# Identity products on TensorE between the last output product and the first expert rows

## What is computed

```python
g_idx = jnp.argmax(softmax(ht @ w_group + b_group), axis=-1)        # 1 of 4 groups
e_sel = (ht @ w_expert + b_expert).reshape(T, 4, 8)[tok, g_idx]
top_v, top_i = lax.top_k(e_sel, 2)                                  # 2 of its 8 experts
top_w = softmax(top_v) * g_p[:, None]
...
yr = (jax.nn.silu(xb @ w_gate[e]) * (xb @ w_up[e])) @ w_down[e]     # blocks of 128 rows of one expert
y  = zeros.at[row_tok].add(yr * row_w[:, None])
```

## Time and profile before

| | |
|---|---|
| time, median of 3 runs | 2466.1 us (2462.89 to 2468.29) |
| the profiled execution's own time | 2466.4 us |
| its span from first to last instruction | 2464.8 us |
| mean granted TensorE clock over the span | 0.964 |
| busy share of PE, DVE, ACT, POOL | 92%, 57%, 49%, 31% |

### The profile page before, as it was taken

One profiled execution on the slowest core, in us unless ns is written; L12 is line 12 of the kernel. 1 busy time (PEld: TensorE's weight loads), 2 busy tenths in 40 slices (PEclk: granted clock), 3 DMA queues, 4 the chain that ended last, 5 costly groups with the idle time before them and its releaser, 6 DMA issues. The chain is left out here.

```text
span 2464.8 us, 36702 instructions
## 1 busy us (share of the span) xinstructions
PE 2273.8 (92%) x11342; PEld 1827.2 (74%) x11342; DVE 1392.7 (57%) x3012; ACT 1220.0 (49%) x1644; POOL 758.1 (31%) x685
## 2 busy tenths in 40 slices
PE   7799999997999999999979995799999999999980
PEld 6688889996777777777658884677888888788760
DVE  4353431105777677667346676576655566666663
ACT  4211111114777777777634443565645555656553
POOL 0000000004887787877501112222222222222220
PEclk9999999998999999999989996899999999999995
DMA  8653334225543454434046444699887888988957
GB/s 272 172 205 111 111 136 117 64 65 133 137 113 86 96 135 109 100 87 120 18 162 197 125 129 155 210 356 356 270 273 247 265 259 266 326 290 270 330 147 289
DMA packets 211558, 450.48 MB, mean 183 GB/s; under 512 B 21633, under 2 KB 56577, under 8 KB 207874
## 3 DMA queue, kind: packets, MB, share of 16 engines
q1 hardware_dynamic: 191410, 378.91, 47.0%
q0 software_dynamic: 17744, 61.96, 10.0%
q10 hardware_dynamic: 2304, 8.39, 1.5%
HBM read 347.44 MB, written 101.76 MB: 182 GB/s over the span
## 5 line engine op out<-in xcount | busy, mean ns | idle before, releaser
L1532 DVE TENSOR_TENSOR gu_lo<-gu_raw,gu_hi 128x2048 fp32r<-128x2048 f32 x128 | 293.8, 2295 | 117.7 <-issue 80.7
L719 DVE TENSOR_SCALAR_CACHE_REDUCE p_ring<-ps_s 128x512 f32<-128x512 f32 (+6 forms) x352 | 277.6, 793 | 117.7 <-PE ps_s L790 104.0
L659 POOL TENSOR_TENSOR p_ring<-p_ring 128x512 f32<-128x512 f32 (+2 forms) x192 | 334.5, 1742 | 16.0
L684 ACT ACTIVATE p_ring<-p_ring,shift 128x1152 f32<-128x1152 f32 (+15 forms) x256 | 305.7, 1196 | 17.5 <-DVE shift L735 17.5
L827 PE MATMUL ps_o<-aT,v_st 128*128 128x512 f32 (+3 forms) x640 | 285.5, 530 | 0.0
L673 ACT ACTIVATE aT<-ps_t 128x512 f32<-128x512 f32 (+1 forms) x320 | 169.1, 530 | 164.2 <-PE ps_t L812 163.0
L1609 PE MATMUL ps_g<-gu_hi,xT_lo 128*128 128x512 f32 x720 | 236.0, 409 | 7.5 <-DVE xT_lo L1547 7.5
L1472 ACT ACTIVATE gu_hi<-gu_raw 128x2048 fp32r (+1 forms) x128 | 238.0, 1915 | 9.9 <-PE ps_g L1609 5.1
L1609 PE MATMUL ps_g<-gu_lo,xT_hi 128*128 128x512 f32 x720 | 228.1, 398 | 0.0
L1609 PE MATMUL ps_g<-gu_hi,xT_hi 128*128 128x512 f32 x720 | 227.9, 398 | 0.0
L656 POOL TENSOR_SCALAR p_ring<-p_ring,coef 128x512 f32<-128x512 f32 (+2 forms) x192 | 168.0, 875 | 122.3 <-DVE coef L748 121.9
(11 more groups left out here) (206 smaller groups left out, 4243.1 us busy)
## 6 DMA issues: line engine op xcount, KB each, us to landing
gu_raw<-in_moe_w_gate SPq DMA_DIRECT2D x128, 512.0 KB
gu_raw<-in_moe_w_up SPq DMA_DIRECT2D x128, 512.0 KB
d_raw<-in_moe_w_down SPq DMA_DIRECT2D x64, 1024.0 KB
qk<-stage SPq DMA_DIRECT2D x64, 512.0 KB, 2.8
q_first<-qk SPq DMA_DIRECT2D x64, 256.0 KB, 5.1
q_second<-qk SPq DMA_DIRECT2D x64, 256.0 KB, 5.1
w_raw<-in_w_in_blocks POOLq DMA_DIRECT2D x11, 1024.0 KB, 6.4
k<-qk SPq DMA_DIRECT2D x8, 1024.0 KB, 12.2
```

What stands on the lines that cost most here:

```text
L659: pool.tensor_tensor(p0(r, c0, c1), p0(r, c0, c1), p1(r, c0, c1), ALU.add).then_inc(mixed, 1)
L684: nc.scalar.activation(p, p, ACT.Exp, bias=shift[:, r % 8, m:m + 1], accum_out=sums[:, r % 8, m:m + 1]).then_inc(raised, 1)
L719: ins = nc.vector.tensor_scalar(p(r, k0, k0 + far), ps_s[:, c % 2, 0:far], SCALE, None, ALU.mult, ALU.max, accum_out=top[:, r % 4, m, col: ...
L1532: nc.vector.tensor_tensor(gu_lo[:, j * GC:(j + 1) * GC], raw(half, j), gu_hi[:, j * GC:(j + 1) * GC].bitcast(F32), ALU.subtract).then_inc( ...
```

## The change

TensorE multiplies the 128 x 128 identity, which lies in SBUF for the transposes, by itself, in fp32 and with 128 columns, into the first columns of `ps_a`. Nobody reads the result. `ps_a` is free there: the added wait is for the last reader of the output stage's transposes. The numbers of products are 16 in step 17, 12 in step 18, 24 in step 19, and 56 after the last count. Nothing else is edited.

```diff
+            def fill(count):
+
+                for _ in range(count):
+                    pe.matmul(ps_a[:, 0:P], ident[:, :], ident[:, :], start=True, stop=True)
+
+            FILLS = {TILES + 1: 16, TILES + 2: 12, TILES + 3: 24}
+
             def step(n, par, at):
...
                 else:
+                    if at == TILES + 1:
+                        pe.wait_ge(oT_lo_set, TILES + OT_LO0)
+                    if at in FILLS:
+                        fill(FILLS[at])
                     route(n, at)
                     turn_h2(n, par, at)
 
             steps(pe, step)
             pe.wait_ge(slot_set, TILES + SLOT0)
             pe.matmul(ps_e[:, 0:EXPERTS], ones[:, :], before[:, :], start=True, stop=True).then_inc(counted, 1)
+            fill(56)
```

## The result

| | before | after |
|---|---|---|
| median of 17 runs each | 2465.45 us (2461.07 to 2468.35) | 2471.68 us (2465.68 to 2474.49) |
| ratio of the times | | 1.0023, 95% interval 1.0016 to 1.0031 |
| span of the profiled execution | 2464.8 us | 2470.3 us |
| mean granted TensorE clock | 0.964 | 0.967 |

A forecast was written before the change was run, and what follows sets the result against it. The pipeline's drain was taken as a chain through VectorE, PE and GpSimd. From 2466.4 us, -1.0 + 0.2 - 0.9 - 0.3 = -2.0 gave 2464.4, and a median 0.3 lower 2464.1 us; range 2460.5 to 2468.5.

The forecast's parts named there:

- 56 fills ... I put +0.2: Behind the last count: fills last 13.8 of 14.0 us with 3.6 us at half clock first; +0.2 us put down.
- Do the fills fit?: TensorE's idle times after each count: at full clock all four groups fit, with 3.3, 1.0, 1.9 and 2.0 us to spare.
- -0.9 for turn_x at full clock: Block 0: eight transposes take 0.91 us instead of some 1.8 at half clock; -0.9 us, bounds 0 and -0.9.
- What one fill costs: Each 128-column fp32 identity product on TensorE: 0.215 us at full clock, 0.43 at half.
- The clock falls again in step 17, and comes back in the 12 fills: TensorE: half clock near 1505 in the first route, full again in step 18's fills after 3.6 us of dense work.
- Counts at full clock, -1.0: Tiles 14 and 15: count start to VectorE's place takes 0.75 us, not 1.27; -1.0 us for both.
- The rows of block 1 bound gate_up's gain: Block 0's gate_up 1.7 us faster, but block 1's rows are late; -0.3 us, PE then idle 1 to 2 us.
- The rival "slower": All groups: identity products do not lift the clock, each fill takes 0.43 us; +14.5 us, median 2480.6, chance 0.05.
- The rival "the clock holds all the way": Drain through the first block: full clock throughout; -4.9 us, median 2461.2, chance 0.17.

The follow-up runs named there:

- e6: Kernel before, no fills, but TensorE waits for three split weight slots of expert 0 ahead of its first x_turned increment; 2468.64 us, ratio 1.0025.
- e1: Changed kernel with all 108 products, but TensorE's first x_turned increment moved ahead of the 56 fills; 2462.46 us, ratio 0.9996.
- e5: e1 with 28, 12, 8 plus 30, and 10 products in steps 17 to 20, and 54 behind the last count; 2457.33 us, ratio 0.9983.
- e10: e1 with 28 products in step 17 in place of 16; 2464.43 us beside 2468.5 for the kernel before, ratio 0.9984.
- e2: Changed kernel without the 56 fills, keeping the groups of 16, 12 and 24; 2463.77 us, ratio 0.9999 to the kernel before.
- e4: Changed kernel with 20 products in place of 56 in the last group, x_turned increment still behind it; 2459.47 us, ratio 0.9984.
- e8: e4 with the x_turned increment moved ahead of the last group of 20; 2459.59 us, ratio 0.9987 to the kernel before.
- e7: Changed kernel with only the last group of 56, x_turned increment ahead of it, no fills in steps 17 to 20; 2462.73 us, ratio 1.0001.
- e9: e5 with 20 products in place of 54 behind the last count; 2464.76 us beside 2468.5 for the kernel before, ratio 0.9982.

## Why the prediction was wrong, step by step

- **The step that failed** is the term "56 fills ... I put +0.2", and with it the question "Do the fills fit?". I measured the gap up to TensorE's own next wait, turn_x at 1544.78, and asked only whether the fills end before it. I did not ask which increments stand behind the fills on the queue. There the limit is GpSimd's list load, for which the credit must be given some 5.4 us after the last count (1535.51 - 1530.13) and not 14.0. It came 8.7 us late; with 0.8 gained by the counts and 1.8 by the shorter issue of the gather, 6.4 arrived at turn_x. e6 shows the loss without fills, e1 its absence with them. Even with the credit early the +0.2 was too small: in e1 the 56 fills take 15.16 us, not 13.8, since the clock stayed at half for 5.1 us of them and not 3.6, and turn_x comes 0.8 us later after the last count than before.
- **A knock-on:** my -0.9 for turn_x at full clock fell with it, since the engine idled again, for 5.85 us. In e1, with turn_x in 1.04 us, a part of it is there: turn_x of block 0 starts no earlier than before, yet that of block 1 comes 66.56 us after the route of tile 13, before 67.12.
- **What one fill costs.** 0.215 us predicted. In e5 54 fills last 12.30 us and 12 last 2.92, so one more fill is 0.223. Right within 4%.
- **The clock falls again in step 17, and comes back in the 12 fills.** Right: half from 1503.1, full from 1510.0. The reason was half right. I blamed thin work as much as idleness; in e1 the clock was down 0.7 us before the thin route began, and in e10, with the gap cut to 0.36 us, the same route ran at full clock. The Trainium skill (TensorE: Matmul & The Clock Gate, Why this matters for your kernels) ties the loss to idle gaps between bursts. Step 17 of e1 and of e10 agree with that; the fall of e10 at 1514.9, after a thin route between 0.17 us and 0.7 us of idleness, does not follow from it.
- **Counts at full clock, -1.0:** -0.8 in the profiled execution. e1, e2, e4 and e8 have the same three groups and gave -0.8, +0.4, +0.5 and -0.6: in e2 and e4 the 24 fills began at half clock and lasted 8.3 us, not 7.0, so the count of tile 15 came behind them.
- **The rows of block 1 bound gate_up's gain:** in e1, with gate_up mostly at full clock, PE waited 0.35 us for them. The place was right, the wait smaller than the 1 to 2 us that I named.
- **The rival "slower"** had the right sign and the wrong place. Products of the identity do lift the clock (e7, at 1532.2), so its mechanism is out. Its own threshold was also miscounted: by 0.43 and 0.215 a fill, 56 fills fill 14.0 us once 3.9 us of them run at half clock, not 9; and the first group, 6.9 us at half clock, does not fit its 6.7. The late increment was not among the rivals.
- **The rival "the clock holds all the way"**, -4.9 us, is what e5 does once the gaps are full: 4.2 by the ratio (0.0017 x 2463.3), 5.9 by the medians.

**Left open in part:** why e4 and e8 are 3 to 4 us faster by their medians than e2 and e1. Counted from the route of tile 13, turn_x of block 2 comes 3.2 us earlier than before in e8 and 1.8 in e4, but only 0.7 in e1 and 0.0 in e2. Most of it arises between the blocks: in e4 and e8 turn_x of block 2 came 12.2 and 12.8 us after that of block 1, before 15.6. In e8 the list landed 0.7 us sooner, and the issue of the gather took 0.99 us, before 2.65. GpSimd's rows and VectorE's, first of e8 and then of the kernel before:

```profile
1561.65 0.58 POOL L1437 DMA_DIRECT2D lists<-slots  x1 [8.54 <-PE ps_x L1608]
1566.32 0.99 POOL L1439 DMA_INDIRECT xg<-h_rows,lists  x1 [4.09 <-DMA lists<-slots]
1563.93 2.29 DVE L1545 TENSOR_TENSOR gu_lo<-gu_raw,gu_hi 128x2048 fp32r<-128x2048 f32 x1 [0.70 <-ACT gu_hi L1485]
1566.55 2.29 DVE L1545 TENSOR_TENSOR gu_lo<-gu_raw,gu_hi 128x2048 fp32r<-128x2048 f32 x1 [0.32 <-DVE gu_lo L1545]
```
```profile
1563.87 0.58 POOL L1424 DMA_DIRECT2D lists<-slots  x1 [8.30 <-PE ps_x L1596]
1569.27 2.65 POOL L1426 DMA_INDIRECT xg<-h_rows,lists  x1 [4.82 <-DMA lists<-slots]
1568.76 2.29 DVE L1532 TENSOR_TENSOR gu_lo<-gu_raw,gu_hi 128x2048 fp32r<-128x2048 f32 x1 [0.33 <-DVE gu_lo L1532]
```

The rows show what goes with a long issue: VectorE's splitting of a weight slot (`gu_lo` or `d_lo`, some 2.3 us each). Before, the gather starts inside such a split (1568.76 to 1571.05) and its issue ends at 1571.92, 0.87 us behind it; in e8 it starts in the gap between two. So it is for block 0: before, the gather at 1538.42 starts inside the split of 1538.03 to 1540.32 and ends 0.89 behind it; in the changed kernel it starts at 1545.02, when no split runs, and takes 1.02. The 12 traces have 552 of these gathers. The 345 that start outside a split take 0.99 to 1.02 us, and so do seven that start at its very edge (in its last 0.13 us, and one 0.03 us after it began); the issue of each of the other 200 ends 0.86 to 0.89 us behind the split. No run moved a split on purpose, so that the one waits for the other is read from these rows and not tested. Why the list lands sooner in e8 is open, and e9 does not have this gain: its gather of block 2 starts 0.16 us into a split and takes 2.99.

## What to carry to other kernels

Work that fills an idle engine's gap delays everything behind it on that engine's queue, and semaphore increments that cost nothing are the easiest to miss: list each increment behind the new work, find who waits for it, and take the earliest of these as the end of the gap. Give one-time credits before any such filler. And in step 17 filler meant to hold the clock paid only when it covered the gap nearly whole: 16 products in a gap of 6.7 us gave nothing in that step, 28 gave 2.3 us.

## What the runs showed of the hardware

Products of the identity by itself bring TensorE's clock back: in e7 it had been at half for 29.6 us when the fills began, behind 2.69 us of idleness and one small product, and it rose 4.6 us into them. The issue of one gather of 128 rows on GpSimd took 0.99 to 1.02 us when no weight split ran on VectorE, and otherwise ended about 0.9 us behind the split that ran when it started, so that it took up to 3.1 us. The late gather of block 0 met no split, and was 1.8 us cheaper than the punctual one, which did.
